# Residual row tails by token halves over three units, with the first transposes ahead of the last unit

## The reference

```python
h = h + rms_norm(mixed, mix_post_g)          # border 1: after w_out
hn = rms_norm(h, ffn_pre_g)                  # feeds w_gate, w_up
h = h + rms_norm(ff, ffn_post_g)             # border 2: after w_down
xn = rms_norm_2(h, norm1_g[l])               # feeds w_in of the second block
h = h + merged @ w_o[l]                      # border 3: after w_o
hn = rms_norm_2(h, norm2_g[l])               # feeds peer_wq
```

## Time and profile before

| what | value |
|---|---|
| median of 3 runs | 2163.53 us (2162.57 to 2166.33) |
| profiled execution, first to last instruction | 2161.6 us |
| PE busy | 2121.7 us, 98% |
| DVE, ACT, POOL busy | 67%, 40%, 48% |
| border 1, end of `wo` | about 229 us |
| border 2, end of `wd` | about 601 us |
| border 3, end of `wo2` | about 923 us |

### The profile page before, as it was taken

How to read it: one execution, slowest core, us unless ns; L and a number is a source line. 1 busy time by engine, 2 the same in 40 slices (tenths; PEclk the granted TensorE clock), 3 DMA queues, 4 the chain that set the end, 5 groups by cost and what they waited for, 6 DMA issues and landing times.

```text
span 2161.6 us, 29125 instructions
## 1 busy us (share of the span) xinstructions
PE 2121.7 (98%) x10648; PEld 1837.8 (85%) x10648; DVE 1442.4 (67%) x2713; ACT 858.3 (40%) x1306; POOL 1038.6 (48%) x573
## 2 busy tenths in 40 slices
PE   8989999999999999999999999999999999999999
PEld 7857888888877877899999999999998888888887
DVE  5973411110054995369998777787867999999987
ACT  4354522232264454253334444444433333333332
POOL 1203244443423333435566888888863444444342
PEclk9999999999999999999999999999999999999999
DMA  4202344444442222334347899998899999999996
GB/s 177 82 27 62 104 117 127 117 119 115 117 118 74 86 71 77 117 106 121 112 147 207 242 267 321 284 315 249 261 309 318 388 388 371 373 375 377 369 359 251
DMA packets 240489, 444.14 MB, mean 205 GB/s; under 512 B 102459, under 2 KB 152028, under 8 KB 240220
## 3 DMA queue, kind: packets, MB, share of 16 engines
q1 hardware_dynamic: 152060, 299.07, 41.8%
q0 software_dynamic: 55488, 134.83, 19.3%
q10 hardware_dynamic: 32800, 8.39, 1.8%
HBM read 397.71 MB, written 44.50 MB: 205 GB/s over the span
## 4 chain that ended last, share of the span: by engine, by line
PE 69%; POOL 13%; DVE 8%; issue 4%; DMA 3%; ACT 2%; SPq 0%; DVEq 0%; ACTq 0%; POOLq 0%
PE bank L469 22%; PE bank L473 22%; PE bank L472 22%; POOL gate_matrices L1151 9%; POOL y L1160 4%; DMA y<-in_peer_u_rows,gidx 3%; DVE m L1979 1%; PE bank L923 1%; DVE xn L1980 1%; DVE WL L2297 1%; PE bank L645 1%; DMA wraw<-in_peer_u 1%; ACT sc L1302 1%; DVE y L2308 0%; DVE hots L2329 0%
## 5 line engine op out<-in xcount | busy, mean ns | idle before, releaser
L1140 POOL TENSOR_TENSOR WL<-wraw,WH 128x1024 fp32r<-128x1024 f32 x171 | 435.9, 2552 | 723.5 <-ACT WH L1191 723.5
L1191 ACT ACTIVATE WH<-wraw 128x1024 fp32r<-128x1024 f32 x411 | 435.0, 1060 | 627.4 <-PE bank L469 393.6
L469 PE MATMUL bank<-XH,WH 128*128 128x384 f32 (+2 forms) x1864 | 668.8, 359 | 12.6 <-DVE WL L2297 7.8
L473 PE MATMUL bank<-XH,WL 128*128 128x384 f32 (+2 forms) x1864 | 657.8, 353 | 0.0
L472 PE MATMUL bank<-XL,WH 128*128 128x384 f32 (+2 forms) x1864 | 657.6, 353 | 0.0
L469 PEld LDWEIGHTS bank<-XH,WH 128*128 128x128 f32 x1864 | 351.4, 189 | 46.3 <-issue 12.9
L472 PEld LDWEIGHTS bank<-XL,WH 128*128 128x128 f32 x1864 | 351.6, 189 | 29.0 <-issue 0.7
L473 PEld LDWEIGHTS bank<-XH,WL 128*128 128x128 f32 x1864 | 351.1, 188 | 28.7
L2297 DVE TENSOR_TENSOR WL<-wraw,WH 128x1024 fp32r<-128x1024 f32 x240 | 293.0, 1222 | 57.6 <-ACT WH L1191 51.8
L469 PE MATMUL bank<-WH,GH 128*128 128x512 f32 x768 | 298.9, 389 | 1.6 <-issue 1.6
L473 PE MATMUL bank<-WH,GL 128*128 128x512 f32 x768 | 298.8, 389 | 0.0
(11 more groups left out here) (313 smaller groups left out, 2561.8 us busy)
## 6 DMA issues: line engine op xcount, KB each, us to landing
wraw<-in_peer_u SPq DMA_DIRECT2D x128, 512.0 KB
wraw<-in_peer_v SPq DMA_DIRECT2D x128, 512.0 KB
activations<-ac SPq DMA_DIRECT2D x122, 192.0 KB
ar<-activations SPq DMA_DIRECT2D x122, 192.0 KB
gr<-gate_matrices SPq DMA_DIRECT2D x124, 128.0 KB
wraw<-in_w_gate SPq DMA_DIRECT2D x22, 512.0 KB
wraw<-in_w_up SPq DMA_DIRECT2D x22, 512.0 KB
wraw<-in_w_down SPq DMA_DIRECT2D x22, 512.0 KB
```

The lines of the kernel that those rows point to most:

```text
L469: mm = pe.matmul(out, wh, xh, start=first, stop=False)
L473: return pe.matmul(out, wl, xh, start=False, stop=last)
L1140: pool.tensor_tensor(WL[:, u % NW, 0:m], wraw[:, u % NR, 0:m], WH[:, u % NW, 0:m].bitcast(F32), ALU.subtract).then_inc(s("w_lo"), 1)
L1191: act.activation(WH[:, u % NW, 0:k * n], wraw[:, u % NR, 0:k * n], ACT.Copy).then_inc(s("w_hi"), 1)
```

## The change

`rows_tail` now runs the last three units of h=1 by token halves: units last-2, last-1, last for tiles 0 and 1, then the same three for tiles 2 and 3, and `turned(n, 0)` stands ahead of the last unit of the second half. `by_halves` and `natural("ci")` therefore no longer begin with it (but for n=0), and their `turned(n, 1)` follows two parts of the first half in place of one. ACT and DVE finish tiles 0 and 1 together, then interleave tiles 2 and 3 with the two halves of `high_half` and `low_half`. The unit last+2 goes from DVE's `NORM_LOWS` to POOL.

```diff
-        NORM_LOWS = [1] + [unit_at[key] + j for key in (("wg", 0), ("ci", 0), ("wq", 0)) for j in (1, 2)]
+        NORM_LOWS = [1] + [unit_at[key] + j for key in (("wg", 0), ("ci", 0), ("wq", 0)) for j in (2,)]
...
-                turned(n, 0)
+                if n == 0:
+                    turned(n, 0)
                 if between:
                     between()
                 for i in range(len(keys)):
                     part(i, 0)
-                    if i == (0 if n else 1):
+                    if i == 1:
                         turned(n, 1)
...
             def rows_tail(name, outs, xs, last, made):
-                for t in range(NT):
-                    rows_part(name, 1, last - 1, outs, xs, last, made, (t,), t == 0)
-                    rows_part(name, 1, last, outs, xs, last, made, (t,), t == NT - 1)
+                first, second = tiles_of(0), tiles_of(1)
+                for i in (last - 2, last - 1, last):
+                    rows_part(name, 1, i, outs, xs, last, made, first, i == last - 2)
+                for i in (last - 2, last - 1, last):
+                    if i == last:
+                        turned(made[1] + 1, 0)
+                    rows_part(name, 1, i, outs, xs, last, made, second, i > last - 2)
...
-                for i in range(last - 1):
+                for i in range(last - 2):
                     rows_part(name, 1, i, outs, xs, last, made)
...
                 if name == "ci":
-                    turned(2, 0)
                     outs = [take(name, t) for t in tiles_of(0)]
                     part(0, tiles_of(0))
+                    part(1, tiles_of(0), False)
                     turned(2, 1)
-                    part(1, tiles_of(0), False)
                     outs += [take(name, t) for t in tiles_of(1)]
... ACT, rows_and_norm:
-                cast_to((name, 1, last), 1)
-                for t in range(NT):
+                def second_half(t):
                     if j < 2:
                         row_square(j, 1, t)
                         row_root(j, t)
-                    if t:
-                        norm_root(n, t - 1)
+                cast_to((name, 1, last), 0)
+                for t in tiles_of(0):
+                    second_half(t)
+                for t in tiles_of(0):
+                    norm_root(n, t)
                 cast_to((name, 1, last), 2)
                 high_half(n, 0, gain, range(KD // 2))
-                norm_root(n, NT - 1)
+                second_half(2)
                 high_half(n, 0, gain, range(KD // 2, KD))
-                cast_to((name, 1, last), 3)
+                second_half(3)
                 if n == 3:
                     (the four copies of the subkeys)
+                for t in tiles_of(1):
+                    norm_root(n, t)
+                cast_to((name, 1, last), 3)
                 high_half(n, 1, gain)
... DVE, rows_and_norm:
-                for t in range(NT):
+                def second_half(t):
                     if j < 2:
                         gained(j, 1, t)
                         add_rows(j, t)
                     else:
                         add_directly(1, t)
-                    if t:
-                        scale_rows(n, t - 1)
+                for t in tiles_of(0):
+                    second_half(t)
+                for t in tiles_of(0):
+                    scale_rows(n, t)
                 low_half(n, 0, gain, range(KD // 2))
-                scale_rows(n, NT - 1)
+                second_half(2)
                 low_half(n, 0, gain, range(KD // 2, KD))
-                for j in range(2):
-                    low(NORM_LOWS[2 * (n - 1) + j + 1], s("w_norm"))
+                second_half(3)
+                for t in tiles_of(1):
+                    scale_rows(n, t)
+                low(NORM_LOWS[n], s("w_norm"))
                 low_half(n, 1, gain)
```

## The result

| comparison | kernel before, median | changed kernel, median | ratio, 95% interval |
|---|---|---|---|
| first (4 runs each) | 2164.93 us | 2181.13 us (2174.23 to 2184.44) | 1.0063 [1.0045, 1.008] |
| second (35 and 12 runs) | 2168.91 us (2161.25 to 2181.53) | 2170.94 us (2166.79 to 2182.11) | 1.0022 [1.0004, 1.0041] |
| third (17 and 12 runs) | 2170.96 us (2161.61 to 2176.04) | 2172.73 us (2165.44 to 2178.27) | 1.0013 [0.9996, 1.003] |

By the first comparison the kernel is slower by 0.63%, and its 2181.13 us lie 10.9 us above 2170.2, where the forecast's range ends. The two longer comparisons, made to see how much of that stays, give 0.22% and 0.13%, the latter not to be told from no change.

What follows compares the result with a forecast made beforehand. PE's list was taken to set the pace, with ACT's and DVE's serial row work binding at the borders. Border terms +0.7 - 0.9 - 3.4 made it 3.6 us longer, 2167.1 us; range 2165 to 2169 widened to 2162.8 to 2170.2.

Steps and rivals of the forecast that it cites:

- Border 1: First border (n=1): PE stalls of 0.7, 0.5, 2.0 and 0.9 us, in all a gain of 0.7 us.
- The cast of last+2: ACT at border 1: ahead of the first `XH`, it waits for the last unit's second half, eating most of 3 us.
- Border 2: Second border (n=2): new 3.3 us PE stall before the second transposes, waiting for tile 3; a loss of 0.9 us.
- Border 3: Third border (n=3): stalls of 1.0 and 1.8 us at the subkeys, 0.8 us after the second transposes; loses 3.4 us.
- PE's clock falls in the new 3.3 us hole of border 2: Rival, chance 0.04: at 1.2 GHz each matmul takes 0.47 us, every 10 us so spent cost 5; 2172 us.
- the sum: Over the three borders, +0.7 - 0.9 - 3.4: 3.6 us longer, 2167.1 us, 0.17% slower.
- work as meant: Rival, chance 0.06: all three borders run through without PE waiting, 9 us less, 2154.5 us.
- the subkeys' banks: Rival, chance 0.12: these banks at border 3 cost little, that border is level, -0.2 us net, 2163.7 us.
- SP's later loads: At borders 1 and 2, SP's loads wait longer, but their data is used later still; costed at nothing.
- the lock: Rival, chance 0.08: DVE's addition and POOL's `WL` hold a shared SBUF port against each other at borders 1 and 2; 2171.3 us.
- the margin forecast: At the borders, 0.7 us between the end of POOL's `WL` (20.5) and DVE's next addition (21.2).
- the bound of 2.1: Other bound for DVE standing beside POOL's `WL`: 2.1 us for each of borders 1 and 2; zero was taken.

Runs made afterwards that it cites:

- order experiment: Changed kernel with all eight `XH` and `XL` of each border ahead of tiles 2 and 3, the cast left where it is: 2176.18 us, ratio 1.0036.

## Why the prediction was wrong

- **Border 1: right.** Stalls of 0.7, 0.5, 2.0 and 0.9 us were forecast and are 0.56, 0.38, 1.82 and 0.71; the border gains 0.72 where 0.7 stood. The cast of last+2 does eat the early transposes' lead (2.41 us of idle ACT).
- **Border 2: the wait right, its price too small.** 3.3 us forecast, 3.14 found. Where the clock holds (hole filled, or by chance in the order experiment) the border costs 0.65 to 0.67, forecast 0.9. In the kernel itself it costs 2.3.
- **Border 3: the same.** 1.0, 1.8 and 0.8 us forecast, 0.83, 1.51 and 0.62 found. With the waits filled the border costs 3.17, forecast 3.4; in the kernel 4.7.
- **The step that failed** is the rival "PE's clock falls in the new 3.3 us hole of border 2 (0.04): no gap of 2.1 us lowered it". It stood at nothing in the sum, and of border 3's waits the clock was not asked at all. It falls in all three executions of the changed kernel, at borders 2 and 3, and costs 1.7 + 1.5 = 3.2 us (the rival had 5 us for border 2 alone). The reason given came from one execution: behind two of the seven holes of 2.10 us the clock did fall. Without the falls the borders give -0.72 + 0.67 + 3.17 = 3.1 us, where the sum was 3.6; with them 6.3, or 0.29%, inside the intervals of the second and (just) the third comparison.
- **The range failed for a second reason.** With 6.3 us in it the sum would have said 2169.8, still below 2170.2. The range was built from errors of the steps around one profiled execution, while the kernel before alone ran from 2160.79 to 2181.53 us in later comparisons; the three runs from which I forecast spanned 3.8 us. The 10 us that the first comparison has beyond the borders' 6.3 lie, in its profiled run, in the stage of the scatters and ahead of border 1. That its four runs fell high, and the four of the kernel before low, by chance is likely from the two later comparisons, not shown; the cause stays open. That those two come out at 0.22% and 0.13%, around the forecast's 0.17%, doesn't bear out the sum either: their intervals hold 3.6 and 6.3 us alike.
- **The other rivals** fall by the same rows: PE waits at border 1 (it doesn't work as meant), and the subkeys' banks are dear, 3.7 us by the experiment that frees them first and by the one that moves the cast.
- **At nothing, and right:** SP's later loads (332.81 and 210.22 us are unchanged), and the lock in the changed kernel: POOL's remainder ran from 233.33 to 235.72 and DVE's addition at 236.40 took 1.28 us. The 0.7 us between them was the margin forecast; the experiments that used it up paid 0.7 us and 1.3 us for it at each border, below the bound of 2.1.

## What to carry to other kernels

When work is reordered so that one engine comes earlier, list what that engine meets next: here the transposes came 3 us sooner, and the gain went to an in-order wait on ACT, to rows that DVE finished no sooner, and to PSUM banks whose release had been put behind other work. Price a new hole of PE at its length plus the slow restart, with a chance, since the same hole brought one in some executions and not in others. To cut a hole in two is no sure cure: 1.60 and 0.61 us left the clock alone in one execution, 0.83 and 1.51 lowered it in three. And before a forecast of 0.2%, look at how widely runs of one kernel spread: three runs that agree within 4 us don't bound it.

## What the runs showed of the hardware

The clock's fall depends on the execution as well as on the hole. By the longest hole at a border, over the thirteen profiles:

| longest hole of PE, us | clock fell to 0.50 behind it |
|---|---|
| 2.90 to 3.14 | 5 of 6 |
| 2.72, 2.40, 2.21 | yes, no, yes |
| 2.28, between borders 2 and 3, where no kernel differs | 6 of 13 |
| 2.10, behind one of 1.11 | 2 of 7 |
| 1.82 to 1.91 | 2 of 7 |
| 1.51, behind one of 0.83 | 3 of 3 |
| 1.52 to 1.60, with others up to 0.70 | 0 of 3 |
| none over 0.62 | 0 of 10 |

Each of the six falls between borders 2 and 3 made that stretch 1.60 to 1.70 us longer.

The Trainium skill, TensorE: Matmul & The Clock Gate, Part 1, says of the clock's rise at a kernel's start that its point varies from run to run, since what the chip watches doesn't start anew with the kernel. That equal holes lower the clock in one execution and not in the next would fit this; no run here moved that phase by itself, so the reason is not shown.
